# Probabilities times values in two passes instead of three, with the two row halves added behind

## The chip, the cores and the metric

The kernel runs on one core of a Trainium2 chip. The metric is the device time of one execution in microseconds. The kernel before was timed three times: median 3029.79 us, from 3029.40 to 3030.63.

## The reference

Two blocks of a model work on 512 tokens (and 256 context tokens) of width 1024. The first has four layers (pooling, neighbourhood attention, convolution, pooling), the second two layers of attention, Fourier mixing, spatial gating and an MLP. What the change touches is one product in the attention of both:

```python
# first block, 16 heads of 64: local keys and 256 context keys
p = jax.nn.softmax(logits, axis=-1)
o = einsum('bhrqik,brikhd->brqhd', p_blk, vb) + einsum('bhrqc,bchd->brqhd', p_ctx, vc)
# second block, two layers, 8 query heads, 2 key/value heads of 64
p = jax.nn.softmax(s, axis=-1)
return einsum('bkgqt,btkd->bqkgd', p, v)
```

All inputs are float32, and the kernel keeps near float32 precision out of rounded matmuls.

## The kernel before, in words

Activations lie transposed, channels on the 128 partitions, tokens along the free dimension. A float32 matrix is split into a rounded part (`_hi`, type float32r) and its rest (`_lo`), and a product is made in three passes: hi by hi, hi by lo, lo by hi. `plan()` writes a list of steps by hand, and TensorE (PE), ScalarE (ACT), VectorE (DVE) and the DMA queue (SP) each walk through that list in its order and do their part of each step. There is no scheduler: the order is the order of the list. Two pieces of PSUM called `turns` are used in turn, and a step may write its turn only when the reader of the turn two before is done (`free_turn`). A piece `scores` has two banks, freed the same way. ScalarE opens its part of a step with waits for everything that VectorE (`s.d0`) and ScalarE (`s.a0`) finished in earlier steps. `give` and `take` hand pieces between the two engines within a step.

Attention goes by blocks of 128 queries, n = 0, 1, 2, ... A head is 64 channels, half of the partitions, and two heads (or two key/value heads) share a tile, `half` 0 and 1. For each n there are the steps `scores` (probabilities before the softmax), `trans` (probabilities turned so that keys lie on the partitions) and `soft`. `soft` does the maximum and the exponential of a later block's scores and rounds the turned probabilities of block n into `pt_hi` with their rest in `pt_lo`. For each even n there are the two steps of the product: `pvmm` on TensorE (line 904 in the first block, 908 in the second), which multiplies the values `v_hi`, `v_lo` of both heads (128 channels, the stationary side) by the probabilities of 256 queries, and `pv`, which keeps the 64 rows of the wanted head and throws the others away. In the first block `pv` is a multiplication with the gate into `pv_tmp` (VectorE), a rounding (ScalarE, line 1091) and a rest (VectorE). In the second it is a rounding (ScalarE, line 1093) and a rest. In the first block half a unit of projection matmuls for the next pair of heads (line 745) stands in each step; the second block has no such filler, and there a turn is shared by the transposes of step n and the product of step n - 4. `vtrans` turns the values and splits them (line 1064 on ScalarE).

The VectorE operations are recorded at the lines of small helpers: 1187 is any tensor_tensor, 1190 any scalar_tensor_tensor, 745 any three-pass matmul, 737 matmuls without a use that keep the clock up.

Of the kernel before, what the change touches and what calls it, by code (L numbers as in the profile page):

```python
# [18 lines left out]
P = 128  # L19
# [73 lines left out]
def plan():  # L93
# [5 lines left out]
    def add(kind, **a):  # L99
        s = Step(kind, **a)  # L100
        s.i = len(steps)
        steps.append(s)
        return s
# [116 lines left out]
    def na_pv(n):  # L220

        mm = add("pvmm", nk=NT, has_turn=True, na=True, qt=n % 4)
        mm.after = [soft[n + 1], vt]
        return mm
# [62 lines left out]
    for L in range(2):  # L287
# [105 lines left out]
        def s_pv(n):  # L393
            mm = add("pvmm", nk=todo[n][3])
            mm.pt = n // 2 % 2
            mm.after = [soft[n + 1], vt]
            return mm
# [84 lines left out]
def build_blocks(nc, A, out):  # L482
    steps, n_units, results = plan()
    with ExitStack() as ctx:
# [43 lines left out]
        def arena(name, shape, dt, off):  # L528
            return sb(name, shape, dt, ar + off)
# [11 lines left out]
        Vh, Vl = arena("v_hi", [P, NT, P], F32R, 64 * K1), arena("v_lo", [P, NT, P], F32R, 67 * K1)  # L541
# [161 lines left out]
        def _(pe):  # L703
# [86 lines left out]
            for s in steps:  # L790
# [103 lines left out]
                elif s.kind == "pvmm":  # L894
# [3 lines left out]
                    if s.na:  # L898

                        wide = NA_CHUNKS[s.qt + 1 if s.qt == 0 else s.qt]  # L900
                        for n, k in enumerate(wide):
                            q = slice(0, 256) if n < 4 else slice(P, 256) if s.qt == 0 else slice(0, P)
                            for j, (v, p) in enumerate(((Vh, PTh[0]), (Vh, PTl[0]), (Vl, PTh[0]))):
                                ins = pe.matmul(PS[:, b, TT + q.start:TT + q.stop], v[:, k, :], p[:, n, q], start=n + j == 0,
                                                stop=n == len(wide) - 1 and j == 2)
                    for n in range(0 if s.na else s.nk):
                        for j, (v, p) in enumerate(((Vh, PTh[s.pt]), (Vh, PTl[s.pt]), (Vl, PTh[s.pt]))):
                            ins = pe.matmul(PS[:, b, TT:TT + 256], v[:, k0 + n, :], p[:, n, :], start=n + j == 0,  # L908
                                            stop=n == s.nk - 1 and j == 2)
# [40 lines left out]
        def _(act):  # L950
            given, taken, own = [0], [0], [0]

            def give(ins):

                given[0] += 1
                ins.then_inc(for_dve, 1)

            def take():

                taken[0] += 1  # L960
                act.wait_ge(for_act, taken[0])
# [27 lines left out]
            for s in steps + [None]:  # L989
# [72 lines left out]
                elif s.kind == "vtrans":  # L1062
                    scores_in(1, s)
                    give(act.activation(Vh[:], SP_[:, 1, 0:TT].rearrange("p (n f) -> p n f", f=P), ACT.Copy))
# [22 lines left out]
                elif s.kind == "pv":  # L1087
                    r = slice(64 * s.half, 64 * s.half + 64)
                    if s.na:
                        take()  # L1090
                        give(act.activation(blocks(Oh[r, s.tile, :], s.q0), paired(PVT[r, :]), ACT.Copy))
                    else:
                        give(act.activation(Hh[r, s.tile, s.q0:s.q0 + 256], ps[r, TT:TT + 256], ACT.Copy))
# [66 lines left out]
        def _(dve):  # L1160
# [106 lines left out]
            for s in steps:  # L1267
# [113 lines left out]
                elif s.kind == "vtrans":  # L1381
                    scores_in(1, s)
                    take()
                    done(rest(Vl[:], SP_[:, 1, 0:TT].rearrange("p (n f) -> p n f", f=P), Vh[:]))
# [38 lines left out]
                elif s.kind == "pv":  # L1423
                    r = slice(64 * s.half, 64 * s.half + 64)
                    q = slice(s.q0, s.q0 + 256)
                    if s.na:
                        give(stt(PVT[r, :], ps[r, TT:TT + 256], 0.5, G2[r, s.pair % 2, q], ALU.mult, ALU.mult))
                        take()
                        done(rest(blocks(Ol[r, s.tile, :], s.q0), paired(PVT[r, :]), blocks(Oh[r, s.tile, :], s.q0)))
                    else:  # L1430
                        take()
                        done(rest(Hl[r, s.tile, q], ps[r, TT:TT + 256], Hh[r, s.tile, q]))
# [242 lines left out]
```

## Time and profile before

| | |
|---|---|
| median of three runs | 3029.79 us |
| profiled execution | 3024.0 us, span 3022.2 us |
| granted TensorE clock, mean | 0.97 |
| TensorE busy | 2833.2 us (94%) |
| VectorE busy | 1726.9 us (57%) |
| ScalarE busy | 938.2 us (31%) |
| product matmuls, first block (line 904) | x480 |
| product matmuls, second block (line 908) | x624 |

Matmul durations overlap each other, so the start of one to the start of the next says more than a duration. A number in brackets at the end of a timeline row is how long the engine stood idle before it, and the arrow names what released it.

### The profile page before, as it was taken

The numbers are of one execution on the slowest core, as the hardware profiler recorded it, in microseconds if no ns is written. First come the engines' busy times: TensorE is split into PE (matmuls) and PEld (weight loads), VectorE is DVE, ScalarE is ACT, GpSimd is POOL, SyncE is SP. The second block draws the span as 40 slices with busy tenths as digits, with TensorE's granted clock in tenths as the row PEclk, the third lists the DMA queues.
The fourth block names the chain that finished last, engine by engine and source line by source line (L and its number), as shares of the span: only waits on it lengthen the run. The fifth ranks groups of instructions, "written<-read, shape, count | busy, mean of one in ns | idle before, by whom it ended". The sixth has DMA issues, their size and how long they took to land.

```text
span 3022.2 us, 37489 instructions
## 1 busy us (share of the span) xinstructions
PE 2833.2 (94%) x14714; PEld 2357.6 (78%) x14714; DVE 1726.9 (57%) x2717; ACT 938.2 (31%) x1440; POOL 0.2 (0%) x4
## 2 busy tenths in 40 slices
PE   7998899999999987998899999999999899999999
PEld 6777777778877865776778878888888668878887
DVE  5786666666567878775556564433234546554343
ACT  2222334444232221332334332212122344333222
POOL 0000000000000000000000000000000000000000
PEclk8999999999999998998999999999999999999999
DMA  5242323333245644422300123322222120123333
GB/s 217 84 141 91 127 88 121 120 121 114 70 153 181 188 124 123 139 86 78 125 1 1 47 94 126 126 77 63 64 63 67 44 70 1 36 83 91 97 92 104
DMA packets 81630, 290.07 MB, mean 96 GB/s; under 512 B 9520, under 2 KB 12592, under 8 KB 80944
## 3 DMA queue, kind: packets, MB, share of 16 engines
q1 hardware_dynamic: 81456, 287.69, 29.4%
q8 instruction: 117, 1.92, 0.3%
q14 instruction: 57, 0.47, 0.0%
HBM read 285.56 MB, written 2.10 MB: 95 GB/s over the span
## 4 chain that ended last, share of the span: by engine, by line
PE 43%; DVE 4%; ACT 2%; issue 1%; DVEq 0%; ACTq 0%
PE turns L745 34%; PE turns L908 3%; PE scores L870 2%; PE turns L890 2%; PE turns L940 1%; DVE tmp L1190 1%; DVE h_lo L1190 1%; DVE pt_lo L1187 1%; ACT pt_hi L1074 1%; DVE tmp L1187 0%; ACT tmp L1085 0%; DVE softmax_diag L1421 0%; PE scores L834 0%; DVE softmax_stats L1401 0%; PE scores L842 0%
## 5 line engine op out<-in xcount | busy, mean ns | idle before, releaser
L745 PE MATMUL turns<-h_hi,w_hi 128*128 128x512 f32 (+1 forms) x2480 | 804.5, 374 | 71.2 <-DVE w_lo L1187 52.9
L745 PE MATMUL turns<-h_hi,w_lo 128*128 128x512 f32 (+1 forms) x2480 | 784.3, 366 | 0.0
L745 PE MATMUL turns<-h_lo,w_hi 128*128 128x512 f32 (+1 forms) x2480 | 782.9, 365 | 0.0
L745 PEld LDWEIGHTS turns<-h_hi,w_hi 128*128 128x128 f32 x2480 | 426.0, 193 | 178.7 <-DVE w_lo L1187 64.9
L745 PEld LDWEIGHTS turns<-h_hi,w_lo 128*128 128x128 f32 x2480 | 422.8, 192 | 76.6
L745 PEld LDWEIGHTS turns<-h_lo,w_hi 128*128 128x128 f32 x2480 | 423.4, 193 | 73.3 <-issue 1.0
L1187 DVE TENSOR_TENSOR w_lo<-w_raw,w_hi 128x1024 fp32r<-128x1024 f32 x300 | 366.7, 1222 | 141.5 <-ACT w_hi L986 141.5
L986 ACT ACTIVATE w_hi<-w_raw 128x1024 fp32r<-128x1024 f32 x300 | 315.4, 1052 | 383.8 <-PE turns L745 363.4
L1190 DVE SCALAR_TENSOR_TENSOR x_lat<-turns,modulation,x_lat 128x512 f32<-128x512 f32 x112 | 84.0, 750 | 337.3 <-PE turns L745 337.3
L745 PE MATMUL turns<-m_hi,w_lo 128*128 128x512 f32 (+1 forms) x768 | 233.3, 358 | 0.0
L745 PE MATMUL turns<-m_hi,w_hi 128*128 128x512 f32 (+1 forms) x768 | 232.4, 357 | 0.0
L745 PE MATMUL turns<-m_lo,w_hi 128*128 128x512 f32 (+1 forms) x768 | 231.9, 356 | 0.0
L1201 DVE CUSTOM_DVE_ANT_0 ada_raw<-ada_raw,cond_rows,ada_bias 128x1024 f32<-128x1024 f32 x176 | 225.2, 1280 | 2.2 <-DMA ada_raw<-in_adapack 1.3
L1187 DVE TENSOR_TENSOR tmp<-tmp 128x768 f32<-128x768 f32 (+4 forms) x88 | 76.5, 870 | 253.9 <-ACT m_hi L1157 253.1
L737 PE MATMUL scores<-dft,ones 128*128 128x256 f32 x500 | 133.5, 415 | 15.9 <-DMA pool_edges<-in_edge 15.9
L745 PEld LDWEIGHTS turns<-m_hi,w_hi 128*128 128x128 f32 x768 | 126.6, 188 | 23.4
L745 PEld LDWEIGHTS turns<-m_lo,w_hi 128*128 128x128 f32 x768 | 126.7, 188 | 22.9
L745 PEld LDWEIGHTS turns<-m_hi,w_lo 128*128 128x128 f32 x768 | 127.2, 188 | 22.0
L1156 ACT ACTIVATE tmp<-turns 128x768 f32<-128x768 f32 (+1 forms) x64 | 45.1, 705 | 292.0 <-PE turns L745 290.2
L1128 ACT ACTIVATE tmp<-x_lat 128x512 f32<-128x512 f32 x56 | 35.4, 632 | 290.3 <-DVE x_ctx L1190 158.9
L737 PEld LDWEIGHTS scores<-dft,ones 128*128 128x128 f32 x500 | 99.9, 208 | 29.4 <-DMA pool_edges<-in_edge 15.9
L1201 DVE CUSTOM_DVE_ANT_0 ada_acc<-ada_raw,cond_rows,ada_bias 128x1024 f32<-128x1024 f32 x88 | 112.5, 1279 | 0.9
(212 smaller groups left out, 3363.9 us busy)
## 6 DMA issues: line engine op xcount, KB each, us to landing
w_raw<-in_wpack SPq DMA_DIRECT2D x300, 512.0 KB, 3.6
ada_raw<-in_adapack SPq DMA_DIRECT2D x176, 512.0 KB, 4.4
bias<-in_bias SPq DMA_DIRECT2D x16, 896.0 KB, 4.7
ada_first_a<-in_adapack SPq DMA_DIRECT2D x12, 512.0 KB, 8.5
x_lat<-in_xT SPq DMA_DIRECT2D x1, 2048.0 KB, 9.4
x_ctx<-in_ctxT SPq DMA_DIRECT2D x2, 1024.0 KB, 9.1
ada_first_b<-in_adapack SPq DMA_DIRECT2D x4, 512.0 KB, 15.3
cond_rows<-in_crow SPq DMA_DIRECT2D x4, 512.0 KB, 10.4
```

What stands on the lines that cost most here:

```text
L737: pe.matmul(dst, ONES[:], CS[:], start=True, stop=True)
L745: ins = pe.matmul(dst[:, lo:lo + sz], w, x[:, lo:lo + sz], start=first and n == 0, stop=last and n == 2)
L870: ins = pe.matmul(SP_[:, s.st, lo:lo + sz], x[:, q], y[:, lo:lo + sz], start=n == 0, stop=n == 2)
L890: ins = pe.matmul(dst[:, c], EX[s.eb][:, c], DIAG[:, s.eb, :], start=True, stop=True)
L908: ins = pe.matmul(PS[:, b, TT:TT + 256], v[:, k0 + n, :], p[:, n, :], start=n + j == 0, stop=n == s.nk - 1 and j == 2)
L940: ins = pe.matmul(PS[:, b, 0:TX], AB[:, n, s.m, j * P:j * P + P], tab[:, n, :], start=n + j == 0, stop=n + j == 4)
L986: act.activation(Wh[:, w % 2, :], RAW[:, w % 2, :], ACT.Copy).then_inc(w_rounded, 1)
L1128: ins = act.activation(T1[:, lo:lo + sz], xseg(lo, m), ACT.Square)
L1156: chain(act.activation(T1[:, 0:t], ps[:, 0:t], ACT.Relu))
L1187: return dve.tensor_tensor(dst, x, y, op)
L1190: return dve.scalar_tensor_tensor(out=dst, in0=x, scalar=c, in1=y, op0=op0, op1=op1)
L1201: ins = dve.tensor_tensor_reduce(dump, ADR[:, n % 2, :], CROW[:, c, :], 0.5, ADAB[:, sect, k:k + 1], ALU.mult, ALU.add, MOD[:, sect, c, k: ...
```

## The change

`v_hi` and `v_lo` (each 128 wide) become one array `v_hi_lo`, with one 128 wide block per head: the head's 64 rounded columns at their place, and the 64 rests in the other half. `pvmm` then multiplies this block by `pt_hi` and `pt_lo`: two passes, after which one half of the rows holds the rounded values' product and the other the rests' product. `pv` copies the rests' half from PSUM across to the partitions of the head (ScalarE), adds it to the other half (VectorE), and goes on from the sum. `tmp3` holds the sum in the second block, `pv_tmp` in the first. (The sum also contains rest by rest, which three passes leave out.)

```diff
-            mm = add("pvmm", nk=todo[n][3])
+            mm = add("pvmm", nk=todo[n][3], half=todo[n][1])
...
-        Vh, Vl = arena("v_hi", [P, NT, P], F32R, 64 * K1), arena("v_lo", [P, NT, P], F32R, 67 * K1)
+        VS = arena("v_hi_lo", [P, NT, 2, P], F32R, 64 * K1)
...
-                            for j, (v, p) in enumerate(((Vh, PTh[0]), (Vh, PTl[0]), (Vl, PTh[0]))):
-                                ins = pe.matmul(PS[:, b, TT + q.start:TT + q.stop], v[:, k, :], p[:, n, q], start=n + j == 0,
-                                                stop=n == len(wide) - 1 and j == 2)
+                            for j, p in enumerate((PTh[0], PTl[0])):
+                                ins = pe.matmul(PS[:, b, TT + q.start:TT + q.stop], VS[:, k, s.half, :], p[:, n, q],
+                                                start=n + j == 0, stop=n == len(wide) - 1 and j == 1)
...
-                    give(act.activation(Vh[:], SP_[:, 1, 0:TT].rearrange("p (n f) -> p n f", f=P), ACT.Copy))
+                    v = SP_[:, 1, 0:TT].rearrange("p (n f) -> p n f", f=P)
+                    for h in range(2):
+                        f = slice(h * 64, h * 64 + 64)
+                        ins = act.activation(VS[:, :, h, f], v[:, :, f], ACT.Copy)
+                    give(ins)
...
                 elif s.kind == "pv":
-                    r = slice(64 * s.half, 64 * s.half + 64)
+                    r, of_rest = slice(64 * s.half, 64 * s.half + 64), slice(64 - 64 * s.half, 128 - 64 * s.half)
+                    give(act.activation((PVT if s.na else T3)[r, 0:256], ps[of_rest, TT:TT + 256], ACT.Copy))
+                    take()
                     if s.na:
-                        take()
                         give(act.activation(blocks(Oh[r, s.tile, :], s.q0), paired(PVT[r, :]), ACT.Copy))
                     else:
-                        give(act.activation(Hh[r, s.tile, s.q0:s.q0 + 256], ps[r, TT:TT + 256], ACT.Copy))
+                        give(act.activation(Hh[r, s.tile, s.q0:s.q0 + 256], T3[r, 0:256], ACT.Copy))
...
-                    done(rest(Vl[:], SP_[:, 1, 0:TT].rearrange("p (n f) -> p n f", f=P), Vh[:]))
+                    v = SP_[:, 1, 0:TT].rearrange("p (n f) -> p n f", f=P)
+                    for h in range(2):
+                        f, g = slice(h * 64, h * 64 + 64), slice(64 - h * 64, 128 - h * 64)
+                        ins = rest(VS[:, :, h, g], v[:, :, f], VS[:, :, h, f])
+                    done(ins)
...
                     q = slice(s.q0, s.q0 + 256)
+                    take()
+                    sums = (PVT if s.na else T3)[r, 0:256]
+                    ins = tt(sums, ps[r, TT:TT + 256], sums, ALU.add)
                     if s.na:
-                        give(stt(PVT[r, :], ps[r, TT:TT + 256], 0.5, G2[r, s.pair % 2, q], ALU.mult, ALU.mult))
+                        chain(ins)
+                        give(stt(PVT[r, :], PVT[r, :], 0.5, G2[r, s.pair % 2, q], ALU.mult, ALU.mult))
                         take()
                         done(rest(blocks(Ol[r, s.tile, :], s.q0), paired(PVT[r, :]), blocks(Oh[r, s.tile, :], s.q0)))
                     else:
+                        give(ins)
                         take()
-                        done(rest(Hl[r, s.tile, q], ps[r, TT:TT + 256], Hh[r, s.tile, q]))
+                        done(rest(Hl[r, s.tile, q], T3[r, 0:256], Hh[r, s.tile, q]))
```

ScalarE in layer 0 of the second block, around one product, in the kernel before (`h_hi` is the rounded attention output, `pt_hi` the rounded probabilities, the exponentials write `tmp`):

```order
L1085 ACTIVATE tmp_64,softmax_stats<-scores,softmax_stats 128x768
L1093 ACTIVATE h_hi<-turns 64x256
L1074 ACTIVATE pt_hi_91<-turns 128x6x128
L1085 ACTIVATE tmp_62,softmax_stats<-scores,softmax_stats 128x768
L1074 ACTIVATE pt_hi_108<-turns 128x6x128
L1085 ACTIVATE tmp_64,softmax_stats<-scores,softmax_stats 128x256
```

The same place in the changed kernel:

```order
L1089 ACTIVATE tmp_64,softmax_stats<-scores,softmax_stats 128x768
L1093 ACTIVATE tmp_63<-turns 64x256
L1098 ACTIVATE h_hi<-tmp_63 64x256
L1078 ACTIVATE pt_hi_107<-turns 128x6x128
L1089 ACTIVATE tmp_62,softmax_stats<-scores,softmax_stats 128x768
```

The copy across the halves now stands ahead of the rounding, and the rounding reads SBUF instead of PSUM.

VectorE in the first block at the border between two pairs of heads, in the kernel before (the softmax step ends with the scaling of `tmp_62`, then come the product's two operations and the split of the values):

```order
L1417 RECIPROCAL softmax_stats<-softmax_stats 128x1
L1419 TENSOR_SCALAR tmp_62<-tmp_62,softmax_stats 128x640
L1190 SCALAR_TENSOR_TENSOR pv_tmp<-turns,na_gate 64x256
L1187 TENSOR_TENSOR o_lo<-pv_tmp,o_hi 64x2x8x16
L1187 TENSOR_TENSOR v_lo<-scores,v_hi 128x768
```

The same place in the changed kernel:

```order
L1426 RECIPROCAL softmax_stats<-softmax_stats 128x1
L1428 TENSOR_SCALAR tmp_62<-tmp_62,softmax_stats 128x640
L1192 TENSOR_TENSOR pv_tmp<-turns,pv_tmp 64x256
L1195 SCALAR_TENSOR_TENSOR pv_tmp<-pv_tmp,na_gate 64x256
L1192 TENSOR_TENSOR o_lo<-pv_tmp,o_hi 64x2x8x16
L1192 TENSOR_TENSOR v_hi_lo<-scores,v_hi_lo 128x6x64 x2
```

An add stands ahead of the gate's multiplication, and the split of the values is two operations. Nothing changes its place relative to other steps.

## Rows read from the trace of the kernel before

**Rows 1.** The page, busy us and share of the span, instructions.

```profile
PE 2833.2 (94%) x14714; PEld 2357.6 (78%) x14714; DVE 1726.9 (57%) x2717; ACT 938.2 (31%) x1440; POOL 0.2 (0%) x4
```

**Rows 2.** One of the three passes, lines 904 and 908: ns min/median/max; group's busy us, mean.

```profile
L904 PE MATMUL turns<-pt_hi,v_lo x160: 273/283/283, 393.6 to 798.2; 128*128 128x256 f32 x128, 128*128 128x128 f32 x32
L908 PE MATMUL turns<-pt_hi,v_lo 128*128 128x256 f32 x208 | 58.7, 282 | 0.0
```

**Rows 3.** Timeline, TensorE, first block: start us, us, engine line op, count.

```profile
592.28 0.39 PE L904 MATMUL turns<-pt_hi,v_hi 128*128 128x256 f32 x1
...
594.09 0.63 PE L887 MATMUL scores<-ident,tmp 128*128 128x128 f32 x4
```

**Rows 4.** Timeline, all engines, border between two pairs of heads.

```profile
597.66 0.55 DVE L1419 TENSOR_SCALAR tmp<-tmp,softmax_stats 128x640 f32<-128x640 f32 x1
598.31 0.43 DVE L1190 SCALAR_TENSOR_TENSOR pv_tmp<-turns,na_gate 64x256 f32<-64x256 f32 x1
598.85 0.41 ACT L1091 ACTIVATE o_hi<-pv_tmp 64x256 fp32r<-64x256 f32 x1 [1.42 <-DVE pv_tmp L1190]
599.30 0.42 DVE L1187 TENSOR_TENSOR o_lo<-pv_tmp,o_hi 64x256 fp32r<-64x256 f32 x1 [0.56 <-ACT o_hi L1091]
599.75 0.81 ACT L1064 ACTIVATE v_hi<-scores 128x768 fp32r<-128x768 f32 x1 [0.49 <-DVE o_lo L1187]
600.69 0.96 DVE L1187 TENSOR_TENSOR v_lo<-scores,v_hi 128x768 fp32r<-128x768 f32 x1 [0.97 <-ACT v_hi L1064]
601.80 0.74 PE L887 MATMUL scores<-ident,tmp 128*128 128x128 f32 x5 [1.52 <-DVE v_lo L1187]
```

**Rows 5.** Timeline, VectorE and TensorE, second and third product of a pair.

```profile
559.45 0.49 DVE L1419 TENSOR_SCALAR tmp<-tmp,softmax_stats 128x512 f32<-128x512 f32 x1
560.45 0.38 PE L866 MATMUL scores<-k_hi,q_hi 64*128 64x256 f32 x1
573.43 0.41 PE L866 MATMUL scores<-k_hi,q_hi 64*128 64x384 f32 x1 [0.97 <-DVE tmp L1419]
574.90 0.82 DVE L1398 CUSTOM_DVE_ANT_0 tmp<-scores,bias 128x640 f32<-128x640 f32 x1
577.92 0.18 PEld L866 LDWEIGHTS scores<-k_hi,q_hi 64*128 64x128 f32 x1 [0.35 <-DVE tmp L1419]
```

**Rows 6.** Timeline, all engines, second block, layer 0, one product.

```profile
1602.36 0.38 ACT L1093 ACTIVATE h_hi<-turns 64x256 fp32r<-64x256 f32 x1 [0.60 <-DVE softmax_diag L1421]
1602.87 0.42 DVE L1187 TENSOR_TENSOR h_lo<-turns,h_hi 64x256 fp32r<-64x256 f32 x1 [0.54 <-ACT h_hi L1093]
1603.43 0.36 PE L908 MATMUL turns<-pt_hi,v_hi 128*128 128x256 f32 x1 [0.17 <-DVE h_lo L1187]
```

**Rows 7.** Timeline, ScalarE, second block, layer 0: the same place, three products apart.

```profile
1600.06 0.81 ACT L1074 ACTIVATE pt_hi<-turns 128x768 fp32r<-128x768 f32 x1 [2.15 <-PE turns L890]
...
1619.59 0.81 ACT L1074 ACTIVATE pt_hi<-turns 128x768 fp32r<-128x768 f32 x1 [2.14 <-PE turns L890]
```

**Rows 8.** Timeline, second block, layer 1, one period.

```profile
2530.25 0.81 ACT L1074 ACTIVATE pt_hi<-turns 128x768 fp32r<-128x768 f32 x1 [2.34 <-PE turns L890]
2532.55 0.38 ACT L1093 ACTIVATE h_hi<-turns 64x256 fp32r<-64x256 f32 x1 [0.60 <-DVE softmax_diag L1421]
2534.09 0.39 PE L908 MATMUL turns<-pt_hi,v_hi 128*128 128x256 f32 x1
2536.35 1.50 PE L890 MATMUL turns<-softmax_diag,tmp 128*128 128x128 f32 x12
2537.97 0.81 ACT L1074 ACTIVATE pt_hi<-turns 128x768 fp32r<-128x768 f32 x1 [2.37 <-PE turns L890]
```

**Rows 9.** Timeline, TensorE, the unit behind the border between two pairs.

```profile
602.94 0.63 PE L745 MATMUL turns<-h_hi,w_lo 128*128 128x512 f32 x1
...
606.25 0.40 PE L745 MATMUL turns<-h_lo,w_hi 128*128 128x512 f32 x1
```

**Rows 10.** Windows: stretch, us, busy PE PEld DVE ACT POOL, clock, DMA, GB/s.

```profile
1605.00:1665.00 60.00, 56.76 (x391) 48.95 (x389) 39.59 (x84) 29.85 (x66) 0.00 (x0) 1.00 0.01 1
```

More of the change, by code:

```diff
@@ L220, in na_pv @@
     def na_pv(n):
-        mm = add("pvmm", nk=NT, has_turn=True, na=True, qt=n % 4)
+        mm = add("pvmm", nk=NT, has_turn=True, na=True, qt=n % 4, half=n % 8 // 4)
         mm.after = [soft[n + 1], vt]
@@ L902, in _ @@
                             q = slice(0, 256) if n < 4 else slice(P, 256) if s.qt == 0 else slice(0, P)
-                            for j, (v, p) in enumerate(((Vh, PTh[0]), (Vh, PTl[0]), (Vl, PTh[0]))):
-                                ins = pe.matmul(PS[:, b, TT + q.start:TT + q.stop], v[:, k, :], p[:, n, q], start=n + j == 0,
-                                                stop=n == len(wide) - 1 and j == 2)
+                            for j, p in enumerate((PTh[0], PTl[0])):
+                                ins = pe.matmul(PS[:, b, TT + q.start:TT + q.stop], VS[:, k, s.half, :], p[:, n, q],
+                                                start=n + j == 0, stop=n == len(wide) - 1 and j == 1)
                     for n in range(0 if s.na else s.nk):
-                        for j, (v, p) in enumerate(((Vh, PTh[s.pt]), (Vh, PTl[s.pt]), (Vl, PTh[s.pt]))):
-                            ins = pe.matmul(PS[:, b, TT:TT + 256], v[:, k0 + n, :], p[:, n, :], start=n + j == 0,
-                                            stop=n == s.nk - 1 and j == 2)
+                        for j, p in enumerate((PTh[s.pt], PTl[s.pt])):
+                            ins = pe.matmul(PS[:, b, TT:TT + 256], VS[:, k0 + n, s.half, :], p[:, n, :], start=n + j == 0,
+                                            stop=n == s.nk - 1 and j == 1)
                     if not s.in_turn:
```

## The prediction, made before the changed kernel was run

> **What bounds the kernel now.** I read the page's totals first, then the busy time by stage, then the timeline of the three attention stages, row by row, with all three engines side by side. TensorE is busy 94% of the span, VectorE 57%, ScalarE 31% [rows 1]; the reader could stop there and credit the whole saving of matmuls. The timeline says otherwise. In the attention stages ScalarE and VectorE are one chain: each step of ScalarE begins with a wait for everything that VectorE has finished before it, and the other way round, so almost nothing of the two overlaps. What counts is where TensorE waits for that chain, and how late the chain may get elsewhere before TensorE does.
>
> The three stages are: the neighbourhood attention of the first block (A, about 390 to 800 us, 32 products of probabilities and values), attention in layer 0 of the second block (B, 1540 to 1697 us, 24 products), and in its layer 1 (C, 2480 to 2607 us, 16 products).
>
> **What is removed.** Of each three passes one goes: a third of the 480 matmuls of line 904 (160, of which 32 are half as wide) and of the 624 of line 908 (208) [rows 2]. Their mean duration, 282 ns, overlaps its neighbours; the pitch is what is saved. Fifteen matmuls of stage A take 592.28 to 594.09, 1.81 us [rows 3], a pitch of 0.12, so five less save 4 x 0.12 + 0.10 = 0.58 us. Eighteen in stage C take 2534.09 to 2536.35, 2.26 us [rows 8]; six less save 6 x 0.119 = 0.71. Work saved on TensorE: A 32 x 0.58 = 18.6, B 16 x 0.71 + 8 x 0.24 = 13.3, C 16 x 0.71 = 11.4; together 43 us.
>
> **What is added.** Behind each product, one ScalarE copy of 64x256 from PSUM, across the partition halves, and one VectorE add of 64x256, both ahead of the pair of operations (round, rest) that stood there. In the second block the old pair goes: ScalarE starts at 1602.36, VectorE 0.51 later and runs 0.42 [rows 6], 0.93 in all. The new four: 0.51 + 0.42 (copy, add), then the hand back and a second round, where the rows of stage A show the same form from SBUF: VectorE ends at 598.74, ScalarE starts 598.85 (0.11), VectorE 0.45 later, 0.42 long [rows 4]. That is 0.51 + 0.42 + 0.11 + 0.45 + 0.42 = 1.91 instead of 0.93: 0.98 more per product, call it d. In stage A the old chain began with a VectorE multiply 0.10 behind the softmax step, of 0.43; now copy 0.05 + 0.51, add 0.42, hand-on 0.05, then the same: 0.94 more.
>
> No row shows an operation that reads one half of the partitions and writes the other. Lower bound of d: the two busy times alone, 0.38 + 0.42 = 0.80, with the hand-offs free. Upper bound: both hand-offs at 0.17 above those read, as much as the shortest to the longest differ, 1.15. I take 0.98, the sum of rows of the same shape. The Trainium skill, page "VectorE: DVE Perf Modes", section on the TRN2 errata for SBUF-source operations, tables VectorE at 120 + N cycles from PSUM and 58 + N from SBUF, for N = 256 an estimate of 0.39 and 0.33 us at 0.96 GHz; by that the second half of the chain would be some 0.1 us cheaper. The rows have 0.42 for either source, so the measurement decides.
>
> The split of the transposed values is cut in two on each engine, ten times. A 128x768 on VectorE is 0.96 [rows 4], a 64x256 0.42, so a fixed part of 0.15; on ScalarE 0.81 against 0.38, a fixed part of 0.17. At most 0.32, less where back-to-back operations overlap, at least nothing; I take 0.14.
>
> **Stage A, one pair of heads after the other (period 54 us).** Each product stands in one of four places.
> - At the border between pairs TensorE waits for the chain: softmax step done 598.21 (597.66 + 0.55), product 598.31 to 599.72, split of the values 599.75 to 601.65, transposes at 601.80 [rows 4]. TensorE's saving is swallowed there; the chain costs 0.94 + 0.14 = 1.08 more. Seven borders: +7.6.
> - At the second place TensorE arrives 0.5 us after the chain (559.94, 560.45) [rows 5]: of 0.58 it keeps 0.42.
> - At the third it waits 0.97 for the softmax step [rows 5], whose chain starts from the unit before: no gain. The product then stands between two softmax steps with nothing to hide it: the next step's maximum, which started at 574.90, starts at 575.84, that step ends at 578.6, and TensorE, there at 577.9 [rows 5], waits until 578.7: +0.8.
> - At the fourth a half unit over all 768 columns stands in front; TensorE arrives 0.6 us or more behind the chain even when that is 0.5 late: the full 0.58 is kept.
>
> Per pair -0.42 + 0.8 - 0.58 = -0.2, seven pairs -1.4. In the last pair matmuls that keep the clock up replace the units; by the same working its losses and gains cancel within 0.2. Stage A: +7.6 - 1.4 = +6, and not -18.6.
>
> **Stage B.** The query tiles come as 6, 6 and 2 chunks of keys; the pattern repeats every three products, 1600.06 to 1619.59, 19.53 us [rows 7]. Walked through once with t = 0 at the end of the first transposes (1599.87): the softmax step ends at 2.45, the product is done at 4.39 (before 3.41), and TensorE, which had waited for it already (0.17) [rows 6], starts the next product at 4.51 instead of 3.53. The chain goes on, 2.62 for the odd step, 2.26 for the even: 9.34, product done 11.28; TensorE starts at 11.40 (before 9.72, where it had 0.28 of slack), 1.42 for 12 matmuls, 0.66 for transposes, 13.48. The odd step ends at 13.59, its scores' maximum (0.96) is ready at 14.64, the exponential can start only then, and that step ends at 16.22; product done 18.16, TensorE 18.28, 1.42 + 1.55, end 21.25. So 21.25 for 19.53: +1.72 per three products. Six whole periods +10.3, the last one with its tail, where the output units wait for the last two products, +2.5. Stage B: +13.
>
> **Stage C.** The period, 2530.25 to 2537.97, is 7.72 [rows 8], all TensorE work. Its ring: product and transposes of an even step (2.26 + 1.43), 0.19 to ScalarE, 2.27 + 0.03 of softmax step, 0.93 of product, 0.12 back: 7.23, so 0.49 of slack. Now 1.55 + 1.43 + 0.19 + 2.30 + 1.91 + 0.12 = 7.50, and TensorE's own work is 7.01. The ring becomes the bound, and of the 0.71 only 0.22 stays: 14 x 0.22, with the tail -3.
>
> **Sum.** +6 + 13 - 3 = +16 us. DMAs, weights and other stages are untouched; each stage hands over through a wait that TensorE ends, so the sum passes through. The profiled execution was 3024.0 us (span 3022.2), the median 3029.8, 5.8 more; I put the difference on the median: 3046 us. With d as the unknown: it counts 21 times in B, 14 in C, 14 in A, so 0.1 us of d is 4.9 us. The bounds 0.80 and 1.15 give 3037 and 3054, and the border splits add up to 2.
>
> **Rivals.**
> - TensorE's work goes and the chain hides in slack: -43 us, 2987. For it: 94% busy. Against it: the rows where TensorE waits, and only 0.49 of slack in C. The point at which it turns is d = 0.65 (16 / 4.9 = 3.3 tenths below 0.98); a milder form, d near 0.5, gives 3046 - 4.8 x 4.9 = 3022, faster than before, if the copy starts ahead of the softmax step's end or the hand-offs are short. The code orders ScalarE's copy behind VectorE's softmax step, so I give both together 0.08, and 0.06 to a sum that lands within 0.2% (6 us, about what a measurement of this kernel can tell from no change).
> - The clock falls. After the waits at the border of stage A seven matmuls of 0.63 us stand where the next have 0.40, with pitches 0.43 and 0.23: 1.4 us lost per fall, to 1.2 GHz from 2.4 GHz [rows 9]. TensorE gets new gaps of 0.4 to 0.7 us in B and C. One fall per three products in B (7) and one per 20 us in C (5) cost 12 x 1.4 = 17 more: 3063. Against it: the waits of 0.3 to 0.5 us in B now go by with no fall (granted clock 1.00 over 1605 to 1665) [rows 10]. Chance 0.10. The Trainium skill, page "TensorE: Matmul & The Clock Gate", section on depth cycling in PSUM queues, states that frequent short idles between groups of matmuls make the clock go up and down; that would be this case. The trace of before bears it out in stage A only.
> - The shifted copy is dear (a half more): d 1.2 or over, 3057. Nothing for or against. Chance 0.06.
>
> **Numbers.** The forecast, 3046, has 0.70 and its own range 3037 to 3054. Reaching to the rivals above and to the flat case, the range is 3033 to 3060. Faster 0.08, same 0.07, slower 0.85.
>
> **What would show it.** Right: ScalarE and VectorE each gain 72 operations of 64x256; the period in B is near 21.2 and in C near 7.5; waits of the products' first matmul for the last VectorE operation of the product before appear three per period in B (0.4 to 0.7 us) and once per period in C; the transposes of stage A wait about 1.1 us longer at seven borders. Wrong: a period in C of 7.0 (TensorE still the bound) or over 7.7, a period in B under 19.5, or matmuls of 0.63 us inside B or C.

## The result, and the profile after

The changed kernel takes 3069.0 us (median of four runs, 3054.3 to 3075.2) beside 3030.2 for the kernel before: 1.0116 times as long, 95% interval 1.0092 to 1.0139. A second lot, six runs beside 28 of before, has 3063.6 against 3029.1, 1.0111 (1.0086 to 1.0136). The intervals are those of the ratio, and the ratio is not quite the quotient of the medians: by it the change costs 35 us, by the medians of the first lot 39. So it is slower, as forecast, but by 35 us and not by 16, and 3069 lies outside the range of 3033 to 3060. Runs of the kernel before differ from one another by up to some 20 us; one source of that is in the last section.

The page of the changed kernel (to be read beside [rows 1]):

```profile
PE 2835.1 (92%) x14346; PEld 2352.7 (77%) x14346; DVE 1756.7 (57%) x2799; ACT 970.5 (32%) x1522; POOL 0.2 (0%) x4
```

TensorE has 368 matmuls fewer (160 + 208) and is yet busy 2 us longer. That alone says that many matmuls ran longer than before. ScalarE and VectorE have 82 instructions more each: 72 for the products, 10 for the split of the transposed values.

The windows of the three attention stages, first of the kernel before, then of the changed one. A goes from its first score product to the first product of the output projection, B from the first score product of the second block in layer 0 to the first MLP product, C from the last Fourier products in layer 1 to the last product with values; B is wider than its 24 products. Columns as in [rows 10], the granted clock behind POOL.

```profile
366.70:798.30 431.60, 404.48 (x2353) 339.96 (x2353) 259.97 (x512) 174.49 (x322) 0.00 (x0) 0.97 0.31 110
1518.60:1852.30 333.70, 316.71 (x1895) 265.26 (x1895) 194.72 (x359) 125.07 (x237) 0.00 (x0) 0.99 0.14 47
2481.20:2606.20 125.00, 122.50 (x854) 106.92 (x853) 77.73 (x138) 60.20 (x108) 0.00 (x0) 1.00 0.00 1
```

```profile
378.00:819.80 441.80, 394.41 (x2193) 327.69 (x2193) 272.69 (x551) 188.60 (x361) 0.00 (x0) 0.94 0.30 108
1542.90:1904.80 361.90, 326.33 (x1783) 272.50 (x1783) 204.39 (x383) 136.26 (x261) 0.00 (x0) 0.92 0.13 43
2536.10:2657.60 121.50, 112.84 (x758) 96.73 (x757) 83.87 (x153) 66.39 (x123) 0.00 (x0) 0.99 0.00 1
```

Read the second column, the length: A +10.2 (forecast +6), B +28.2 (forecast +13), C -3.5 (forecast -3). Together +34.9, as much as the ratio gives. The profiled executions differ by 51: a further 11.3 stand ahead of A, where both kernels do the same work, and 5 between the stages. A second profile of the changed kernel (e12 below) has +9.0, +21.9 and -3.4, together +27.5, and again some 10 ahead of A. A stage that two kernels have in common differs between executions too, by up to 1.5 us in A and 3.7 in B (table below). In B TensorE has 112 matmuls fewer and is busy 9.6 us longer, at a clock of 0.92 instead of 0.99.

Inside B the timeline of the changed kernel shows the new chain and what it does to TensorE. Two of the products follow each other here, their copies at 1640.42 and 1647.24 (rows left out at the dots and between):

```profile
1640.42 0.38 ACT L1093 ACTIVATE tmp<-turns 64x256 f32<-64x256 f32 x1 [1.03 <-DVE softmax_diag L1430]
1640.93 0.42 DVE L1192 TENSOR_TENSOR tmp<-turns,tmp 64x256 f32<-64x256 f32 x1 [0.55 <-ACT tmp L1093]
1640.96 0.51 PE L870 MATMUL scores<-sk_lo,sq_hi 64*128 64x512 f32 x2
1641.39 0.42 ACT L1098 ACTIVATE h_hi<-tmp 64x256 fp32r<-64x256 f32 x1 [0.58 <-DVE tmp L1192]
1641.84 0.42 DVE L1192 TENSOR_TENSOR h_lo<-tmp,h_hi 64x256 fp32r<-64x256 f32 x1 [0.48 <-ACT h_hi L1098]
1642.29 0.81 ACT L1078 ACTIVATE pt_hi<-turns 128x768 fp32r<-128x768 f32 x1 [0.48 <-DVE h_lo L1192]
1642.40 0.35 PE L908 MATMUL turns<-pt_hi,v_hi_lo 128*128 128x256 f32 x1 [0.57 <-DVE h_lo L1192]
...
1647.24 0.38 ACT L1093 ACTIVATE tmp<-turns 64x256 f32<-64x256 f32 x1 [0.55 <-DVE softmax_diag L1430]
1647.35 0.68 PE L870 MATMUL scores<-sk_hi,sq_hi 64*128 64x512 f32 x2 [0.73 <-DVE softmax_diag L1430]
1647.83 0.84 PE L870 MATMUL scores<-sk_lo,sq_hi 64*128 64x512 f32 x2
...
1650.04 0.41 PE L908 MATMUL turns<-pt_lo,v_hi_lo 128*128 128x256 f32 x1
1650.26 0.41 PE L908 MATMUL turns<-pt_hi,v_hi_lo 128*128 128x256 f32 x1
```

From the copy to the end of the last rest it is 1641.84 + 0.42 - 1640.42 = 1.84 us; the forecast had 1.91, against 0.93 before [rows 6]. So d is 0.91 and not 0.98. TensorE waits 0.57 for the chain of the product before and then, 5 us later, 0.73 for the softmax step, and falls to 1.2 GHz: pairs of score matmuls of 0.84 stand where 0.51 stood at 1640.96, and the matmuls of the next product come every 0.21 to 0.22 us instead of every 0.12. By this the next product is late; one period later the waits and the fall are there again.

What TensorE waited for in B, summed (us in total, times, longest), first before, then changed:

```profile
PE turns L908 <- DVE h_lo L1187: 4.2, 9, 1.7
PE scores L870 <- DVE softmax_diag L1421: 2.4, 14, 0.2
```

```profile
PE turns L908 <- DVE h_lo L1192: 17.6, 20, 2.2
PE scores L870 <- DVE softmax_diag L1430: 7.2, 20, 1.1
```

Measured from the copy (or rounding) that opens a product to that three products on, the periods of B were 19.50, 19.52, 19.52, 19.56, 19.54, 19.90 before and are 21.38, 22.60, 23.77, 23.50, 23.50, 23.49 now, and from the second period on one step of each is late by a fall of the clock. C goes by 7.41 per period instead of 7.72 (forecast 7.50), at a clock of 0.99; two copies one period apart:

```profile
2585.38 0.38 ACT L1093 ACTIVATE tmp<-turns 64x256 f32<-64x256 f32 x1 [0.60 <-DVE softmax_diag L1430]
2592.79 0.38 ACT L1093 ACTIVATE tmp<-turns 64x256 f32<-64x256 f32 x1 [0.60 <-DVE softmax_diag L1430]
```

The border of stage A in the changed kernel, to be read beside [rows 4]:

```profile
614.76 0.55 DVE L1428 TENSOR_SCALAR tmp<-tmp,softmax_stats 128x640 f32<-128x640 f32 x1
616.32 0.42 DVE L1195 SCALAR_TENSOR_TENSOR pv_tmp<-pv_tmp,na_gate 64x256 f32<-64x256 f32 x1
617.67 0.87 ACT L1067 ACTIVATE v_hi_lo<-scores 128x384 fp32r<-128x384 f32 x2 [0.49 <-DVE o_lo L1192]
618.68 1.02 DVE L1192 TENSOR_TENSOR v_hi_lo<-scores,v_hi_lo 128x384 fp32r<-128x384 f32 x2 [1.04 <-ACT v_hi_lo L1067]
619.85 1.30 PE L887 MATMUL scores<-ident,tmp 128*128 128x128 f32 x5 [2.14 <-DVE v_hi_lo L1192]
```

From the end of the softmax step (615.31) to the transposes it is 4.54 us, before 601.80 - 598.21 = 3.59: +0.95, forecast +1.08. The transposes themselves now run at 1.2 GHz already (1.30 for five, before 0.74).

### The profile page after: what moved, and what is told of

It reads as the page before. It is cut to its first block and busy times, and to the rows that moved or that the text cites. A ratio compares the mean times of both kernels' runs of the same rounds, so it can differ in the third digit from the quotient of the medians.

```text
span 3073.4 us, 36917 instructions
## 1 busy us (share of the span) xinstructions
PE 2835.1 (92%) x14346; PEld 2352.7 (77%) x14346; DVE 1756.7 (57%) x2799; ACT 970.5 (32%) x1522; POOL 0.2 (0%) x4
## 5 line engine op out<-in xcount | busy, mean ns | idle before, releaser
L745 PEld LDWEIGHTS turns<-h_hi,w_hi 128*128 128x128 f32 x2480 | 428.5, 194 | 184.0 <-DVE w_lo L1192 70.1
L737 PE MATMUL scores<-dft,ones 128*128 128x256 f32 x500 | 140.1, 430 | 15.8 <-DMA pool_edges<-in_edge 15.8
L890 PE MATMUL turns<-softmax_diag,tmp 128*128 128x128 f32 x832 | 116.5, 291 | 0.0
## 6 DMA issues: line engine op xcount, KB each, us to landing
cond_rows<-in_crow SPq DMA_DIRECT2D x4, 512.0 KB, 10.2
```

The source lines that it names most:

```text
L737: pe.matmul(dst, ONES[:], CS[:], start=True, stop=True)
L745: ins = pe.matmul(dst[:, lo:lo + sz], w, x[:, lo:lo + sz], start=first and n == 0, stop=last and n == 2)
L890: ins = pe.matmul(dst[:, c], EX[s.eb][:, c], DIAG[:, s.eb, :], start=True, stop=True)
```

## The experiments

All are the changed kernel with a mode for each product of probabilities and values. Times stand beside the kernel before in the same lot: its medians were 3028.4 (e1 to e4), 3031.8 (e5 to e8) and 3029.1 (e9 to e12). The table has the lengths of the three windows in the profiled execution, with the granted clock in B.

| kernel | ratio, 95% interval | A | B (clock) | C |
|---|---|---|---|---|
| before | | 431.6 | 333.7 (0.99) | 125.0 |
| changed | 1.0116 (1.0092 to 1.0139) | 441.8 | 361.9 (0.92) | 121.5 |
| changed, again (e12) | 1.0111 (1.0086 to 1.0136) | 440.6 | 355.6 (0.94) | 121.6 |
| e1 new chain, three passes | 1.0172 (1.0154 to 1.0190) | 449.4 | 358.1 (0.97) | 132.9 |
| e2 two passes, old chain | 0.9957 (0.9938 to 0.9975) | 435.3 | 326.3 (0.98) | 114.0 |
| e3 changed, one filler | 1.0080 (1.0065 to 1.0096) | 438.9 | 349.8 (0.97) | 122.4 |
| e4 changed, two fillers in B | 1.0103 (1.0088 to 1.0119) | 441.2 | 354.3 (0.97) | 122.4 |
| e5 changed in B alone | 1.0077 (1.0057 to 1.0096) | 433.1 | 359.6 (0.93) | 125.2 |
| e6 changed in C alone | 0.9994 (0.9980 to 1.0007) | 432.6 | 332.4 (0.99) | 121.7 |
| e7 two places of A, and C | 0.9988 (0.9973 to 1.0002) | 428.5 | 330.2 (0.99) | 121.6 |
| e8 rests joined late | 1.0018 (1.0003 to 1.0034) | 435.9 | 344.0 (0.95) | 115.7 |
| e11 late, one filler | 1.0015 (1.0000 to 1.0030) | 437.0 | 340.1 (0.97) | 121.3 |
| e9 places of A, C late | 0.9957 (0.9940 to 0.9974) | 429.3 | 333.9 (0.99) | 115.0 |
| e10 as e9, places late too | 0.9960 (0.9942 to 0.9977) | 427.7 | 333.3 (0.99) | 115.2 |

**The chain alone, and the passes alone.** e1 has the new chain and still three passes (the third repeats the rests of the probabilities instead of taking the rests of the values); e2 has two passes and the old chain, so it leaves the rests of the values out.

```diff
+                v = VS[:, k, s.half, :]
+                los = VS[:, k, :, :].rearrange("p h f -> p (h f)")[:, 64:192]
+                return {"two": [(v, ph), (v, pl)], "pass": [(v, ph), (v, pl)],
+                        "chain": [(v, ph), (v, pl), (v, pl)],
+                        "three": [(v, ph), (v, pl), (los, ph)]}[s.mode]
```

> As changed, but TensorE does three passes again (the third repeats the second, so the product is not the reference's): the longer chain of ScalarE and VectorE with TensorE's old amount of work. Stage lengths in the changed kernel's trace against before: A (neighbourhood attention) +10.2, B (second block, layer 0) +28.1, C (layer 1) -3.5 us. Theory 1 (only the rings of waits count, clock aside): each ring holds the longer product as well, so B loses at least the changed kernel's computed +13 and up to 5 more, +13 to +19; C +7; A +13; sum +33 to +39. Theory 2 (the waits let TensorE's clock fall, and this costs B about 15 us and A about 5): three passes keep TensorE busier, the granted clock in B is near 1.00 instead of 0.91, and B is +13 to +19, so SHORTER than the changed kernel's +28 although it does more work. Rival (the clock falls for another reason, the same in both): B +33.

> Two passes, but the old two operations behind them; the copy across and the add are left out, so the rests' product is missing from the result. It shows what the shorter TensorE work alone brings. Theory 1: A -8 us (only the places where TensorE is the bound keep 0.4 to 0.58 us), B -5 to -8, C 14 x (7.72 - 7.01) = -10, sum about -24 against before. Theory 2 says the same but adds that shorter work means longer waits in B: granted clock below 1.00 there and B at 0 or above. Rival (94% busy means that nearly all of the saving comes out): -43.

Neither expectation came out whole: e1 costs 52 us by the ratio (33 to 39 expected) with the clock of B at 0.97 and not near 1.00, and e2 gains 13 us, not 24.

In C the two parts add up: +7.9 and -11.0 give -3.1, measured -3.5. In B they give +24.4 - 7.4 = +17, measured +28.2 and +21.9: some 5 to 11 us belong to neither part alone. In B the changed kernel, with a third of e1's product matmuls gone, is no shorter than e1 (361.9 and 355.6 beside 358.1). Three periods of e1 have no fall and take 21.75 us; without falls the changed work takes 20.95, as e3 below shows, so the falls take back what the passes save.

In A the chain alone costs 17.8, and the passes alone, which take only work away, make the stage 3.7 us longer (2.2 beside the longest of three executions with that stage unchanged, 431.6, 432.6 and 433.1). Together that would be +21.5, but the changed kernel has +10.2 and +9.0: behind the longer chain the removed passes save 7.6 us (449.4 to 441.8), behind the old one nothing. The trace of e2 shows how the latter comes about; this is the third product of a pair in e2, to be read beside 573.43 in [rows 5]:

```profile
416.90 0.39 PE L759 MATMUL turns<-h_hi,w_lo 128*128 128x512 f32 x1
418.85 0.41 PE L880 MATMUL scores<-k_hi,q_hi 64*128 64x384 f32 x1 [1.56 <-DVE tmp L1454]
...
420.58 0.77 PE L759 MATMUL turns<-h_hi,w_hi 128*128 128x512 f32 x1
421.15 0.63 PE L759 MATMUL turns<-h_lo,w_hi 128*128 128x512 f32 x1
421.58 0.63 PE L759 MATMUL turns<-h_hi,w_lo 128*128 128x512 f32 x1
```

TensorE is there 0.6 us sooner, the softmax step is not, the wait grows from 0.97 to 1.56, and behind it matmuls of 0.63 us follow where 0.40 stood. Of the seven such waits six have such a stretch behind them, and one, at 474.84, has not. That the longer wait is the cause of it is a reading of these rows; no run changed that wait alone. The windows of e2 for A and B:

```profile
374.10:809.40 435.30, 397.79 (x2193) 330.44 (x2193) 260.77 (x520) 175.92 (x330) 0.00 (x0) 0.94 0.30 109
1530.60:1856.90 326.30, 305.13 (x1782) 254.58 (x1782) 194.24 (x359) 125.74 (x237) 0.00 (x0) 0.98 0.15 48
```

**The wait filled with unused products.** If the forecast of the chain's price lacked the clock, matmuls whose result nobody reads (fillers), put where TensorE waits, must give some of it back.

```diff
+                    if s.in_turn and FILL[s.layer]:
+                        wait_steps([s.prev_soft])
+                        for _ in range(FILL[s.layer]):
+                            pe.matmul(PS[:, b, 0:256], ONES[:], CS[:], start=True, stop=True)
```

> The changed kernel with one matmul without use (float32, 256 columns, 0.46 us at full clock) ahead of each product within attention of the second block, at the place where TensorE waits for the product before. Theory 1: the filler lies in a wait, nothing changes, B +28, C -3. Theory 2: the waits of 0.6 to 1.3 us in B shrink by 0.46; the granted clock in B rises above 0.91 and B comes down by 5 to 15 us; C unchanged within 2.

> As e3, but two such matmuls (0.92 us) in layer 0 and one in layer 1. Theory 2: clock in B at or near 1.00 and B at +13 to +17 us: the computed +13, plus up to 4 because the filler is longer than two of the three waits of a period. Theory 1 without the clock: B at +28 plus 4.

One filler per product makes B 12 us shorter (361.9 to 349.8; 6 against the second profile of the changed kernel) though it adds work, and the clock stands at 0.97. From its fourth period to its sixth e3 has no fall, 20.97, 20.95, 20.97; here is one of them, three products apart:

```profile
1643.51 0.38 ACT L1115 ACTIVATE tmp<-turns 64x256 f32<-64x256 f32 x1 [0.60 <-DVE softmax_diag L1456]
...
1664.46 0.38 ACT L1115 ACTIVATE tmp<-turns 64x256 f32<-64x256 f32 x1 [0.60 <-DVE softmax_diag L1456]
```

20.95 us for the period at 2.4 GHz (forecast 21.25, less 3 x 0.07 for the smaller d). Its first three periods still hold two falls. The second filler (e4) gives nothing more: a step without a fall takes 7.64 us instead of 7.34, and every second period still has a fall (steps of 9.23, 9.21 and 9.22). B is 354.3 there, where 347 to 351 was expected. So more filler is not simply fewer falls.

**One stage at a time.**

```diff
-NA_MODE, L0_MODE, L1_MODE, FILL = {0: 'two', 2: 'two', 4: 'two', 6: 'two'}, 'two', 'two', 0
+NA_MODE, L0_MODE, L1_MODE, FILL = {0: 'three', 2: 'three', 4: 'three', 6: 'three'}, 'two', 'three', 0
```

> Two passes and the added halves stand in the second block of layer 0 alone (24 products); the neighbourhood attention and layer 1 keep three passes over the same stationary store and the old order of ScalarE and VectorE. Theory (the longer chain and a lower granted clock): the stretch from the first score product of that block to the first MLP product grows by 28 us as it did in the changed kernel (333.7 to 361.9), its granted clock near 0.92, and the time is about 3028 + 27 = 3055. Rival 1 (the chain alone, as forecast): +13 in that stretch at a clock of 0.99, time 3041. Rival 2 (the clock falls there only because the neighbourhood attention before it had left TensorE less busy): with that stage as before the clock stays above 0.97 and the stretch grows by 13 to 17 us, time 3041 to 3045.

> Two passes and the added halves in the second block of layer 1 alone (16 products). Every theory: that stretch 125.0 to 121.5 us, so the time is 3.5 us below before, about 3025, at a clock of 0.99 to 1.00. It tells whether a stage's own change adds up with the others: if the time is 3028 or more, the gain seen in that stage of the changed kernel is lost outside it.

e5, windows of A and B:

```profile
368.60:801.70 433.10, 404.98 (x2353) 340.39 (x2353) 260.94 (x520) 175.13 (x330) 0.00 (x0) 0.97 0.30 110
1526.10:1885.70 359.60, 322.24 (x1783) 268.95 (x1783) 204.34 (x383) 136.02 (x261) 0.00 (x0) 0.93 0.13 43
```

B alone costs 24.9 us by the medians and falls to 0.93 with A untouched at 0.97. Both rivals are out: it is not the chain at full clock alone, and nothing that stage A hands on. e6 gives -1.8 us (-6 to +2) by the medians and 3.3 in the stage: a gain of that size is not to be seen in the time.

**Only where it should pay.** Positions 0 and 4 of eight are the second and fourth product of each pair.

```diff
+NA_MODE, L0_MODE, L1_MODE, FILL = {0: 'two', 2: 'three', 4: 'two', 6: 'three'}, 'three', 'two', 0
```

> Two passes and the added halves only where the forecast's working made them pay: at the second and the fourth product of each pair of the neighbourhood attention (forecast -0.42 and -0.58 us each, 8 pairs, -8 us together) and in the second block of layer 1 (-3.5 us); three passes and the old chain elsewhere. Forecast's working: -11.5 us, time 3017. Theory with the clock: the neighbourhood attention gives less or nothing back, since taking the third pass away there alone already made it 3.7 us longer at a clock of 0.94 instead of 0.97; -4 to +2 us for the whole, time 3024 to 3030.

-3.3 us (-8 to +1), in the windows A -3.1 and C -3.4. The forecast's working for the two places, -8, is out by more than half; as in e2, what TensorE saves comes back as waits ahead of other score products (12 of them instead of 7 in A).

**A shorter chain.** ScalarE rounds the half of the rounded values directly, copies the rests while VectorE subtracts, and VectorE adds them to the small part only.

```diff
+                        give(act.activation(Hh[r, s.tile, s.q0:s.q0 + 256], ps[r, TT:TT + 256], ACT.Copy))
+                        give(act.activation(T3[r, 0:256], ps[of_rest, TT:TT + 256], ACT.Copy))
...
+                        chain(rest(Hl[r, s.tile, q], ps[r, TT:TT + 256], Hh[r, s.tile, q]))
+                        take()
+                        done(tt(Hl[r, s.tile, q], Hl[r, s.tile, q].bitcast(F32), T3[r, 0:256], ALU.add))
```

> Two passes everywhere, but the row half of the rests is joined later. In the second block ScalarE rounds the half of the rounded values as before, copies the half of the rests while VectorE subtracts, and VectorE adds it to the small part only: one VectorE operation of 0.42 us more in the chain, no hand-over more, d about 0.45 instead of 0.90. In the neighbourhood attention the copy lies beside the gate product, the gate product of the rests beside ScalarE's rounding: d about 0.45 too. By the forecast's slope (4.9 us per 0.1 us of d, nothing gained or lost at 0.65): 10 us below before, 3018. With the clock (it falls in the second block of layer 0 when TensorE waits once per product): half way between the two-pass kernel with the old chain and the changed kernel, stage by stage +7, +10 and -7, so 3038 at most; if the clock there stays above 0.97, 3022 to 3028.

> The kernel that joins the rests late everywhere, with one product of 256 columns whose result is not used ahead of each product of probabilities and values in the two second blocks, where TensorE waits. Theory of the clock: as the same filler did in the changed kernel (361.9 to 349.8 at 0.97 instead of 0.92), it lifts the granted clock in layer 0 from 0.95 to 0.97 or more and shortens that stretch from 344.0 to 335 to 339, time 3031 to 3035. Rival (the wait alone, no clock): the filler can only cost, 344 to 350 in layer 0 and 116 to 121 in layer 1, time 3040 to 3050.

The windows of A, B and C in e8:

```profile
371.40:807.30 435.90, 395.69 (x2193) 328.80 (x2192) 284.40 (x582) 188.44 (x361) 0.00 (x0) 0.94 0.30 109
1529.90:1873.90 344.00, 316.43 (x1782) 264.24 (x1782) 204.27 (x383) 134.80 (x261) 0.00 (x0) 0.95 0.14 45
2502.80:2618.50 115.70, 112.30 (x758) 96.81 (x757) 83.55 (x152) 65.76 (x123) 0.00 (x0) 0.99 0.00 1
```

Half the extra chain brings 30 us back by the ratios (1.0116 to 1.0018), but not the 10 us of gain that the forecast's slope gives: at 3039.4 us it lies 1 us beyond the 3038 expected at most. B is still +10, with falls in it. At full clock its period is 19.9 (7.20 + 6.36 + 6.36 in e11), 0.4 above before. C is bound by TensorE's work: 7.00 per period, where the forecast put that work at 7.01. The filler (e11) lifts B to 0.97 and shortens it by 3.9, less than expected (335 to 339), and costs 5.6 in C, where nothing was to be filled.

**A version that is faster than before.** Late joining in C, two passes at the two places of A, B left at three passes.

```diff
+NA_MODE, L0_MODE, L1_MODE, FILL = {0: 'two', 2: 'three', 4: 'two', 6: 'three'}, 'three', 'late', 0
```

> The second and fourth product of each pair of the neighbourhood attention with two passes and the added halves, layer 0 with three passes and the old chain, layer 1 with two passes and the rests joined late. By the stages measured so far: neighbourhood attention -3 us (the run with these places: 428.5), second block of layer 0 at 330 to 334 (0), layer 1 -9 us (the run with the late joining: 115.7): 12 us below before, about 3020 against a median of 3032. If stages do not add up, 3026 to 3032.

> As the run before, but the two places of the neighbourhood attention join the rests late too. If the length of the chain is what those places cost, their stage falls another 2 to 4 us below 428.5, time 3016 to 3018. If the clock that falls where passes are taken away is what limits them, it stays at 428 to 432 and the time is that of the run before.

e9: 3015.2 us (12 runs) against 3029.1, 13.8 us below, interval 8 to 18; by the windows -2.3 in A, 0 in B, -10.0 in C. The product and its chain in C, TensorE at full clock and its first matmul 0.16 us behind the end of the chain, with no wait of its own:

```profile
2530.83 0.38 ACT L1123 ACTIVATE h_hi<-turns 64x256 fp32r<-64x256 f32 x1 [0.61 <-DVE softmax_diag L1461]
2531.24 0.38 ACT L1125 ACTIVATE tmp<-turns 64x256 f32<-64x256 f32 x1
2531.34 0.42 DVE L1223 TENSOR_TENSOR h_lo<-turns,h_hi 64x256 fp32r<-64x256 f32 x1 [0.54 <-ACT h_hi L1123]
2531.79 0.42 DVE L1223 TENSOR_TENSOR h_lo<-h_lo,tmp 64x256 fp32r<-64x256 f32 x1
2532.37 0.39 PE L929 MATMUL turns<-pt_hi,v_hi_lo 128*128 128x256 f32 x1
```

1.38 us from the first operation to the end of the last, 0.45 above before. e10 is 1.6 shorter in A by its windows, no more than A differs from execution to execution, and no shorter in the time: at those places the chain's length is not seen to limit.

> The changed kernel once more, in the same lot as these. Every theory: about 3066, 34 to 40 us above before; by stage (neighbourhood attention, layer 0, layer 1) +10, +28 and -3.5 with the granted clock of layer 0 near 0.92. The first score products of the neighbourhood attention come between 366 and 379 us, by how long the first matmuls of the program run at the half clock: if they come 10 us earlier than in the first profile of the changed kernel, the whole is as much shorter.

The repetition agrees: +9.0, +21.9, -3.4 by stage. B differs by 6 us between two executions of the same kernel, 0.92 and 0.94: five long steps instead of six, and a faster tail. From the end of B to the start of C, where both kernels do the same work, the repetition takes 6 us more than before.

## Why the prediction was right in sign and wrong in size

**The chain.** Right in mechanism, a little too dear. d was 0.91 instead of 0.98, no dear copy across the partition halves (0.38 us, as the plain one), and where the clock held, the steps came out close: C 7.41 for 7.50 and -3.5 for -3; B 20.95 for 21.25; the border of A +0.95 for +1.08. The measured 1.84 us for the chain and the 0.38 for the copy settle that rival.

**The clock: the step that failed.** The forecast gave "the clock falls" a chance of 0.10, against it "the waits of 0.3 to 0.5 us in B now go by with no fall". But the change made just those waits longer and more frequent: from 9 times with 4.2 us in sum to 20 times with 17.6. In the changed kernel each period of B from the second to the seventh has its fall, as the rival said: steps of 8.96, 10.14, 9.87, 9.86, 9.86 and 8.77 us, where the clean ones of e3 have 7.34. That is 57.46 - 6 x 7.34 = 13.4 us, 2.2 per fall. Halved matmuls inside B are what the forecast itself had named as a sign of being wrong. The changed kernel's one step of this kind without a fall, its first, took 7.40. The rival's price, 1.4, was read off a stretch of independent matmuls behind a border [rows 9]; in B the halved matmuls are links of the ring (product, transposes, softmax step), which would explain the dearer fall; no run separates the two. The sum for B: seven periods at full clock 7 x (20.95 - 19.52) = 10.0, falls 13.4, the rest, 4.8, in the last two products and behind them. That rest is not free of the clock either; TensorE is at 1.2 GHz over and behind the last products:

```profile
1736.40:1750.10 13.70, 10.28 (x41) 9.17 (x40) 4.40 (x11) 3.18 (x9) 0.00 (x0) 0.50 0.01 1
```

So the forecast's 13 for B is near 14.8, the sum without the falls in the periods, but partly by luck: six periods at full clock cost 8.6 and not 10.3, the last with the tail 6.2 and not 2.5. The rival's whole time, 3063, came near the measured 3069 and 3064, by luck in part too: it counted five falls in C, whose first twelve steps all take 7.40 or 7.41, priced those in B too low, and left A out.

**Stage A.** Here the price of the chain and the gain of the passes were both worked out at a constant clock. The forecast says of the third place that it waits 0.97 for the softmax step, "whose chain starts from the unit before: no gain". The wait did swallow the saving and grew to 1.56, in e2 and in the changed kernel, and in six pairs of seven of e2 the clock fell behind it (in one of seven in the changed kernel, in none before). So with the old chain the saved passes were worth less than nothing: A +3.7 in e2. In the changed kernel the loss is at the borders. Before, TensorE fell to 1.2 GHz behind five of the seven, and not behind the other two. The 8 us behind one of each kind:

```profile
495.40:503.40 8.00, 8.00 (x50) 6.90 (x51) 5.18 (x8) 4.51 (x7) 0.00 (x0) 1.00 0.01 2
601.80:609.80 8.00, 8.00 (x41) 6.63 (x42) 3.61 (x7) 3.81 (x6) 0.00 (x0) 0.79 0.01 2
```

From border to border it is 52.4 us behind one without a fall and 54.0 behind one with a fall, so a fall there costs 1.6. In the changed kernel the clock falls at all seven, and a pair takes 54.6 to 55.6. Seven waits 0.95 longer and two more falls make 9.9 of the measured 10.2 (an estimate from these rows); the forecast had the longer waits, but no fall that was not there before, and 1.4 of saving on top. At six of the seven the clock also stays down longer. Twenty microseconds from just ahead of the same border, before and changed:

```profile
596.70:616.70 20.00, 17.62 (x98) 14.41 (x97) 11.88 (x24) 8.28 (x16) 0.00 (x0) 0.91 0.12 40
```

```profile
613.80:633.80 20.00, 16.24 (x86) 13.39 (x86) 11.66 (x24) 8.28 (x17) 0.00 (x0) 0.83 0.07 20
```

0.91 is 3.6 us at 1.2 GHz, 0.83 is 6.8. Whether the longer stretch costs more is not shown: pairs take 54.7 to 55.6 us behind the long stretches and 54.6 behind the short one. Waits of the score products of line 866 went from 7 (6.8 us) before to 17 (15.7 us) in the changed kernel.

The Trainium skill, page "TensorE: Matmul & The Clock Gate", section on depth cycling in PSUM queues, says that frequent short idles between groups of matmuls make the clock go up and down. The forecast cited it and held that the trace bore it out in A only; the runs bear it out in B too (granted clock 0.92 and 0.94), and e3, with more matmuls and less time, speaks for the idle time as the cause. That a filler gives back all that the clock took is not shown: two falls remained in e3, and e4 with twice the filler has more.

**The slope.** "0.1 us of d is 4.9 us" and a turning point at 0.65 do not hold once the clock depends on d: with d = 0.45 (e8) it should have been 10 us below before and was 5.5 above.

**What stays open.** Why the clock falls behind six of seven waits of 1.56 us in e2 and behind one of seven in the changed kernel; why B of one kernel has five falls in one execution and six in another; why falls remain with one filler in some periods and with two in every second. And how much of the 35 us the stages make: +34.9 in one profile, +27.5 in the other, while both profiles of the changed kernel also came some 10 us later to A than the one of before, which may be chance (last section).

## What to carry to other kernels

Where TensorE already waits for a chain of two other engines, count a longer chain twice: once as the wait, and once as the matmuls at half speed behind it (here 1.6 us per fall at the borders of A, 2.2 in B). Taking TensorE work away ahead of a wait lengthens the wait first of all and may cost time, as in stage A of e2; it pays surely where TensorE is the bound (here layer 1, 7.72 to 7.00 us per period). And join the small part of a split value late: the rests need only reach the small half, which cuts the added chain from 0.91 to 0.45 us.

## What the runs showed of the hardware that was not expected

Both kernels do the same work up to stage A, yet its first score product comes between 365.7 and 378.7 us in the 14 profiles. Most of the difference arises in the first matmuls of the program, with no idle time in them. The same group of sixteen, before and (two rows) changed:

```profile
21.91 1.84 PE L807 MATMUL turns<-cond_silu,ada_first_a 128*128 128x2 f32 x16
```

```profile
30.45 3.41 PE L807 MATMUL turns<-cond_silu,ada_first_a 128*128 128x2 f32 x16
36.43 1.93 PE L807 MATMUL turns<-cond_silu,ada_first_a 128*128 128x2 f32 x16
```

TensorE begins at half its rate in every profile, with its first matmul at about 16 us, and changes to the full one at 19.1 us in the profile of before and at 36.6 in that of the changed kernel; over the 14 profiles it is 18.8 to 37.2. The clock column does not show it:

```profile
20.00:30.00 10.00, 10.00 (x73) 9.54 (x74) 4.73 (x10) 5.73 (x12) 0.00 (x0) 1.00 1.03 420
```

```profile
20.00:30.00 10.00, 10.00 (x36) 9.04 (x37) 5.08 (x10) 5.38 (x11) 0.00 (x0) 1.00 1.02 419
```

Half as many matmuls, and 1.00 in both. In all 14 profiles the clock's record begins only with that change to the full rate, and the column counts what lies ahead of it as 1.00. So in the first microseconds of a program read the matmuls' distances, not the clock. Why the change comes early or late is open; six of the 14 profiles had it at 19 us, the one of before among them, and both of the changed kernel at 37. Together with the rest of the way to A it gives one execution up to 13 us over another; the windows of the stages do not contain it.

A ScalarE copy from one half of the partitions to the other takes 0.38 us for 64x256, as within one half.
